# Dilated attention's 24 units, laid out as steps between the dense matmuls of two runs

## What is computed

```python
h = rms_norm(x, norm_w)
proj = h @ w_in
a_u, a_v, a_z, b_q, b_k, b_v, b_z, m_q, m_z, g = split(proj)
u = gelu(a_u); vv = layer_norm(gelu(a_v)); y_a = spatial_gating(u, vv) * silu(a_z)

q, k = rms_norm(b_q per head), rms_norm(b_k per head)
for gi, (window, dilation) in enumerate(((128, 1), (512, 4), (2048, 16))):
    # each query attends to t, t-d, ..., t-window; 4 heads of 64
    scores = q @ k.T * 64 ** -0.5 + bias[bucket(distance)]     # masked to the window
    m = max(scores); p = exp(scores - m); l = sum(p)
    o_g, lse_g = (p @ v) / l, m + log(l)
wts = softmax over the groups of lse
y_b = sum(wts * o_g) * silu(b_z)

kv = rms_norm(mem, mem_norm_w) @ m_w_kv          # 256 memory tokens
y_m = softmax(rms_norm(m_q) @ rms_norm(mk).T) @ mv * silu(m_z)
x = x + (gates[0]*(y_a@proj_a) + gates[1]*(y_b@proj_b) + gates[2]*(y_m@proj_m)) @ w_out
```

## Time and profile before

| | us |
|---|---|
| median of 3 runs (1761.26 to 1764.52) | 1763.2 |
| span of the profiled execution | 1759.4 |
| PE busy in it | 1726.5 (98%) |
| DVE busy | 914.9 (52%) |
| ACT busy | 654.1 (37%) |
| first run, up to the end of its gate slots | 0 to 262.7 |
| the stage of the 24 units | 262.7 to 326.4 |
| middle run from its first slot | from 326.4 |

### The profile page before, as it was taken

How to read it: one execution, slowest core, us unless ns; L and a number is a source line. 1 busy time by engine, 2 the same in 40 slices (tenths; PEclk the granted TensorE clock), 3 DMA queues, 4 the chain that set the end, 5 groups by cost and what they waited for, 6 DMA issues and landing times.

```text
span 1759.4 us, 22322 instructions
## 1 busy us (share of the span) xinstructions
PE 1726.5 (98%) x8731; PEld 1398.6 (79%) x8731; DVE 914.9 (52%) x1528; ACT 654.1 (37%) x1225; POOL 249.0 (14%) x412
## 2 busy tenths in 40 slices
PE   7999999999999999999999999999999999999998
PEld 5788887778888888778888788888887777777786
DVE  5158868664336744763222322467242545657764
ACT  5234438611324432752112211233313363434731
POOL 3012210188801100000000000482000000000000
PEclk9999999999999999999999999999999999999999
DMA  4121110346232200311111221242713111001132
GB/s 145 52 76 47 37 37 2 118 144 192 85 123 72 61 25 13 94 30 49 54 42 52 66 63 31 96 144 79 156 31 99 42 31 37 25 25 48 40 130 107
DMA packets 148339, 122.93 MB, mean 70 GB/s; under 512 B 10555, under 2 KB 133898, under 8 KB 147594
## 3 DMA queue, kind: packets, MB, share of 16 engines
q1 hardware_dynamic: 148234, 121.49, 22.9%
HBM read 108.21 MB, written 13.26 MB: 69 GB/s over the span
## 4 chain that ended last, share of the span: by engine, by line
PE 56%; DVE 2%; ACT 1%; issue 1%; DVEq 0%; ACTq 0%
PE psum L93 30%; PE psum L278 10%; PE psum L81 7%; PE psum L2707 2%; PE psum L2738 2%; PE psum L2721 1%; PE psum L1720 1%; PE psum L945 0%; PE psum L931 0%; PE psum L2503 0%; PE psum L2524 0%; PE psum L920 0%; PE psum L2217 0%; DVE ya_low L1572 0%; PE psum L1481 0%
## 5 line engine op out<-in xcount | busy, mean ns | idle before, releaser
L93 PE MATMUL psum<-hT,w_parts 128*128 128x512 f32 x3360 | 796.4, 393 | 7.1 <-PEq L61 3.4
L93 PEld LDWEIGHTS psum<-hT,w_parts 128*128 128x128 f32 x3360 | 629.3, 189 | 144.7 <-issue 8.9
L221 DVE TENSOR_TENSOR w_parts<-w_raw,w_parts 128x1024 fp32r<-128x1024 f32 x88 | 111.7, 1270 | 364.9 <-ACT w_parts L210 364.9
L93 PE MATMUL psum<-h2T,w_parts 128*128 128x512 f32 x1248 | 297.1, 394 | 0.0
L93 PEld LDWEIGHTS psum<-h2T,w_parts 128*128 128x128 f32 x1248 | 230.8, 188 | 48.3 <-issue 1.7
L1514 ACT ACTIVATE gate<-psum,cols 128x512 f32<-128x512 f32 x48 | 33.1, 689 | 284.1 <-PE psum L81 284.0
L81 PE MATMUL psum<-y_high,wp_parts 128*128 128x512 f32 x384 | 128.8, 395 | 0.3 <-DVE ya_low L1572 0.3
L210 ACT CAST w_parts<-w_raw 128x1024 fp32r<-128x1024 f32 x88 | 91.6, 1041 | 24.7 <-DMA w_raw<-w_in 19.5
L81 PEld LDWEIGHTS psum<-y_high,wp_parts 128*128 128x128 f32 x384 | 72.0, 188 | 18.9 <-DVE ya_low L1572 1.6
L278 PE MATMUL psum<-w_parts,y_parts 128*128 128x512 f32 x360 | 82.6, 390 | 0.6 <-DVE w_parts L271 0.6
L403 DVE RECIPROCAL x<-x 128x512 f32<-128x512 f32 x24 | 80.2, 3341 | 0.0
(11 more groups left out here) (377 smaller groups left out, 2298.5 us busy)
## 6 DMA issues: line engine op xcount, KB each, us to landing
w_raw<-w_in SPq DMA_DIRECT2D x188, 256.0 KB, 3.4
middle_a<-ada_w SPq DMA_DIRECT2D x32, 384.0 KB, 3.7
w_raw<-w_out SPq DMA_DIRECT2D x16, 512.0 KB, 3.8
qkT<-x SPq DMA_DIRECT2D x8, 512.0 KB, 7.9
w_raw<-m_w_kv SPq DMA_DIRECT2D x16, 256.0 KB, 3.1
base<-x SPq DMA_DIRECT2D x8, 512.0 KB, 4.0
x_kept<-x_ring SPq DMA_DIRECT2D x8, 512.0 KB, 3.8
base<-x_kept SPq DMA_DIRECT2D x8, 512.0 KB, 3.6
```

Source lines behind the costliest of these rows:

```text
L93: last = pe.matmul(out, lhs(a, k), rhs(b, k), start=(n == 0), stop=(n == len(SLOT) - 1))
L221: dve.tensor_tensor(self.parts[:, u, LO, :, :], self.raw[:, :, :], self.parts[:, u, HI, :, :].bitcast(F32), ALU.subtract).then_inc(self.lo ...
```

## The change

The units' stage is taken apart. What one round of it did (scores(b), turn(b-2), mix(b-3) on PE, and the parts of ACT and DVE) is now a "body" b, 0 to 26. `Dense` gets four places in a slot: after matmul 6, 12, 18 and 24. Bodies 0 to 14 stand in the gate slots 36 to 39 of the first run (from place 1 of slot 36), bodies 15 to 26 in slots 0, 1 and 2 of the middle run. With it:

- scores have one pair of banks, `(2,)` (banks 2 and 3), so that scores(b) waits for the maxima of b-1; there is one `pT`; the `p` buffers lie in `x1` and, later, in dead rows of `qkT`;
- the gate tiles keep to banks 0 and 1, the last key tile to 6 and 7;
- on DVE and ACT the bodies of places 0 to 2 stand ahead of everything else of their slot, that of place 3 behind it;
- the first tile of the middle run is split after the last slot of the first run's tile 18, in the run itself;
- `Join` starts at slot 3 and spreads one group a slot instead of one half; `Modulation` moves from slot 1 to 4, its sum from 19 to 22; `MemNorm` from 18 to 21 with 3 slots a step in place of 4; the inputs of `SsmMatrices` are loaded at slot 3, its save moves from 30 to 32;
- short tiles start one tile later, and the last two of them now stand together behind the last query tile.

```diff
@@ class Dense, tensor
-            slot_part(pe, out, lhs, rhs, range(8))
+            slot_part(pe, out, lhs, rhs, range(6))
+            for work in self.beside:
+                work.tensor_body(pe, s, 0)
+            slot_part(pe, out, lhs, rhs, range(6, 8))
...
                 work.tensor_mid(pe, s)
+                work.tensor_body(pe, s, 1)
...
                 before.after(pe, self, s - 1)
+            for work in self.beside:
+                work.tensor_body(pe, s, 2)
             last = slot_part(pe, out, lhs, rhs, range(18, 24))
@@ class Dense, scalar
         for s, slot in enumerate(self.slots):
...
+            for place in range(3):
+                for work in self.beside:
+                    work.scalar_body(act, s, place)
...
                 w.split_high(act, slot.n // 2 + 1, slot.n % 2)
+            elif slot.last and slot.n + 2 == len(self.tiles) and self.ahead:
+                self.ahead.ahead_high(act)
             for work in self.beside:
                 work.scalar(act, s)
+                work.scalar_body(act, s, 3)
@@ class Dense, vector
         for s, slot in enumerate(self.slots):
+            for place in range(3):
+                for work in self.beside:
+                    work.vector_body(dve, s, place)
...
                 w.split_low(dve, slot.n // 2 + 1, slot.n % 2)
+            elif slot.last and slot.n + 2 == len(self.tiles) and self.ahead:
+                self.ahead.ahead_low(dve)
             self.tiles[slot.n].vector(dve, self, s)
             if s:
                 self.tiles[self.slots[s - 1].n].vector_last(dve, self, s - 1)
             for work in self.beside:
                 work.vector(dve, s)
+                work.vector_body(dve, s, 3)
@@ class DilatedAttention
-        super().__init__(core, stack, units, ident, p, pT, (0, 2), 4, (6, 7), lag=2)
+        super().__init__(core, stack, units, ident, p[0], pT, (2,), 4, (6, 7), lag=2)
...
+    def body_pe(self, pe, b):
...
+            self.scores(pe, b)
...
+            self.turn(pe, b - lag)
...
+            self.mix(pe, b - lag - 1)
+
+    def body_act(self, act, b):
+        if 0 <= b - self.lag < self.n:
+            self.move_act(act, b - self.lag)
+        if b < self.n:
+            self.exps(act, b)
+
+    def body_dve(self, dve, b):
...
+        if 0 <= b - self.lag - 2:
+            self.store(dve, b - self.lag - 2)
+        if b < self.n:
+            self.maxima(dve, b)
+        if 0 <= b - self.lag < self.n:
+            self.move_dve(dve, b - self.lag)
@@ class DilatedBodies (new)
+    def body(self, s, place):
+        b = 4 * s + place - self.start
+        return self.first_body + b if b >= 0 and self.first_body + b < self.attention.bodies else None
@@ class Middle
-        for small, tile in zip(mvs[0:3] + mks, late + mqs):
+        for small, tile in zip(mvs[0:2] + mks, late + mqs):
             self.tiles += [small, tile]
-        self.tiles.append(mvs[3])
+        self.tiles += mvs[2:4]
```

More of the change, by code:

```diff
@@ L360, in scalar @@
         sq, high = run.sq[:, 0:self.width], run.sq_high[:, 0:self.width]
+        if q == 0 and run.heads_free:
+            act.wait_ge(*run.heads_free)
         if q >= 1:
@@ L517, in scalar @@
             work.scalar_start(act)
-        if self.heads:
+        if self.heads and not self.same_at:
             act.copy(self.same, self.same_from).then_inc(self.same_made, 1)
@@ L523, in scalar @@
             tile = self.tiles[slot.n]
+            if self.same_at and s == self.same_at:
+                act.copy(self.same, self.same_from).then_inc(self.same_made, 1)
+            for place in range(3):
+                for work in self.beside:
+                    work.scalar_body(act, s, place)
             for work in self.beside:
@@ L853, in tensor, with tensor_before @@
         last.then_inc(self.turned, 1)
+    def tensor_before(self, pe, s):
+        if s == self.run.first_slot(self.run.tiles.index(self.reuses)):
+            for side, kept in enumerate(self.kept):
+                pe.wait_ge(kept, (len(self.pairs) + 1 - side) // 2)
     def place(self, n):
@@ L917, in scores @@
             pe.wait_ge(self.maxed, u - before + 1)
-            pe.wait_ge(self.exped, u - before + 1)
+            if self.units[u - before]["bias"] is None:
+                pe.wait_ge(self.exped, u - before + 1)
         for h in range(4):
@@ L1053 @@
 class DilatedAttention(Attention):
-    def __init__(self, core, stack, units, ident, p, pT, w, before):
-        super().__init__(core, stack, units, ident, p, pT, (0, 2), 4, (6, 7), lag=2)
-        self.w, self.before = w, before
-        assert self.n % 3 == 0
-    def evicted(self, engine, banks):
-        for b in banks:
-            engine.wait_ge(self.before.free[b], max(slot.prior + 1 for slot in self.before.slots if slot.bank == b))
-    def sync_start(self, sp):
-        sp.wait_ge(self.before.w.low, 2 * len(self.before.tiles))
-        self.w.ahead_load(sp)
@@ L1117, in vector_early, with __init__, place, evicted @@
-    def vector_early(self, dve, s):
-        pass
-    def vector(self, dve, s):
-        pass
+    def __init__(self, core, stack, units, ident, p, pT, before, tabled):
+        super().__init__(core, stack, units, ident, p[0], pT, (2,), 4, (6, 7), lag=2)
+        self.places, self.before, self.tabled, self.bodies = p, before, tabled, self.n + self.lag + 1
+        self.ring = 3
+    def place(self, u):
+        return self.places[u // TT][u % self.ring]
+    def evicted(self, engine, b):
+        engine.wait_ge(self.before.free[b], max(slot.prior + 1 for slot in self.before.slots if slot.bank == b))
@@ L1182, with __init__ @@
     ROWS = 96
-    FIRST = 1
-    def __init__(self, core, places_dram, sel_dram, maxima, sums, oT, ybT, ident, room, room_at):
+    FIRST = 3
+    def __init__(self, core, places_dram, sel_dram, maxima, sums, oT, ybT, ident, room, room_at, dilated, loads):
+        self.dilated = dilated
         self.core, self.places_dram, self.sel_dram, self.ident = core, places_dram, sel_dram, ident
@@ L1244, in tensor @@
             pe.transpose(self.by_head(), self.m.rearrange("p g c -> p (g c)"), self.ident).then_inc(self.turned, 1)
[L1245 to L1246 removed]
+        if 2 <= s < 5:
+            g = s - 2
             rows = slice(32 * g, 32 * g + 32)
[L1248 removed]
+            if g == 0:
                 pe.wait_ge(self.chosen, 1)
                 pe.wait_ge(self.rest, 1)
[L1251 to L1259 removed]
+            for pair in range(2):
+                if g:
+                    pe.wait_ge(self.used, 2 * g + pair - 1)
+                for h in range(2):
+                    half = slice(h * HALF, (h + 1) * HALF)
+                    out = bank(self.core, 2 + 2 * pair + h, 1)
+                    pe.matmul(out, self.sel[rows, pair * P:(pair + 1) * P], self.high[rows, half],
+                              start=True, stop=False)
+                    last = pe.matmul(out, self.sel[rows, pair * P:(pair + 1) * P],
+                                     self.low[rows, half], start=False, stop=True)
+                last.then_inc(self.spread, 1)
     def vector_early(self, dve, s):
@@ L1357, in at @@
     def at(self, s, step):
-        t, k = divmod(s - self.first, 4)
-        return {0: t, 1: t - 1}[step // 4] if (k == step % 4 and 0 <= t - step // 4 < 2) else None
+        t, k = divmod(s - self.first - step, 3)
+        return t if k == 0 and 0 <= t < 2 else None
     def sync(self, sp, s):
@@ L3270, in first_block @@
                              1 / 64, order=by_group(rates[j // 2]), banks=four) for j in range(6)]
+            for where, tile in [((6, 7), keys[5])] + [((0, 1), tile) for tile in gates]:
+                tile.banks = (where, where)
             tiles = values + queries + keys + gates
@@ L3295, in first_block @@
         w_gates = SplitTiles(core, stack, [(24, lambda n: gate_tile(order[0], 0))], shares=w)
-        middle.prepare(w_middle, dilated, maxima, sums, oT, ybT, stat, w_gates)
+        middle.prepare(w_middle, dilated, last_bodies, maxima, sums, oT, ybT, stat, w_gates)
         run_dense(core, run, middle.run)
@@ L3373, in __init__ @@
                        for j in range(6)]
-        late, self.tiles = self.tiles[13:16], self.tiles[0:13]
+        late, self.tiles = self.tiles[14:16], self.tiles[0:14]
         for tile in late:
@@ L3390, in __init__, with prepare @@
                                wait=lambda h, j=j: self.turn_av.wait(2 * j + h)) for j in range(6)]
-    def prepare(self, w, dilated, maxima, sums, oT, ybT, stat, ahead):
+    def prepare(self, w, dilated, bodies, maxima, sums, oT, ybT, stat, ahead):
         core, A, later, mergedT, N = self.core, self.A, self.later, self.mergedT, SSM_GROUPS
```

196 lines of the change are left out of this document (102 added, 94 removed).

## The result

The changed kernel takes 1781.8 us (median of 4 runs, 1774.4 to 1784.8), the kernel before 1762.2 beside it (4 runs): ratio 1.011, 95% interval 1.0095 to 1.0126. Slower, by 19.6 us. The profiled execution of after has a span of 1781.1, 21.7 more than before's 1759.4; the prediction had 22.6.

What follows compares the result with a forecast made beforehand. PE, busy 1726.5 of 1759.4 us, was taken as the bound. Terms 0.2 + 8.4 + 2.8 + 2.6 + 3.1 + 1.7 + 3.8 = +22.6 gave span 1782.0, plus 3.8 to the runs' median: 1785.8 us, range 1771 to 1793.

Steps and rivals of the forecast that it cites:

- the clock: Behind the new waits: slow matmuls cost 3.8 us, ends 0 and 7.5; the first wait's share is in the 8.4.
- what I had put at nothing: Other moves, such as the later `SsmMatrices` save: shifts by whole slots that PE does not wait for, no term.
- The ledger: Units' stage on PE: spreading frees 4.9 us, 27 insertions of 0.19 add 5.1; +0.2 us, other end -4.9.
- The first gate slot: PE waits 4.1 us ahead of scores(1), 2.5 ahead of scores(3), for maxima delayed by DVE's reciprocals; +8.4 us in all.
- The splits of slot 37, of the start of the middle run and of slot 1: DVE's weight splits stand ahead of the maxima in these places; PE waits 2.8, 2.6 and 3.1 us.
- The short tiles: Two short tiles at the end: weights of the first `a_v` tile land late, PE waits 1.7 us.
- that sign: Gate slot 38 should take 24 x 0.2285 us plus 4 bodies with 0.19 each, and no wait.
- the case with waits only where no split makes them: Rival: only the reciprocal's 8.4, 0.75 of clock and the short tiles' 1.7 stay; +11.1, 1774.3 us; chance 12%.
- The wait-free case: Rival: maxima come in time everywhere; 1763.4 us, or 1758.3 if insertions cost nothing; chance 5%.
- The case of the clock that holds: Rival: dense matmuls ahead of each wait keep 2.4 GHz; +17.8, 1781.0 us, 1775.9 with free insertions; chance 15%.
- The function switch at twice its load: Rival: on ACT, a silu/exponential switch costs twice the table load, lengthening three split waits; +5.2, 1791.0 us; chance 5%.
- the late chain: Rival: `SsmMatrices` starts late, PE waits for the first memory key's sums; 3 to 8 us more, 1789 to 1794; chance 8%.

Runs made afterwards that it cites:

- experiment 8: Changed kernel, maxima first, short tiles apart, earlier reciprocal pair ahead of the split, low-part split behind body 4, last reciprocal halved: 1762.6 us, ratio 1.0003.
- Experiment 4: Changed kernel with 16 useless dense matmuls on PE just ahead of scores(1): 1778.0 us (one run).
- Experiment 1: Changed kernel with DVE taking the place-3 body ahead of split and reciprocal, the middle run's starting split behind its first body: 1772.5 us, ratio 1.0058.
- experiment 2: Changed kernel with a plain copy for the silu of both gate tiles and the middle run's first two tiles: 1770.6 us (one run).
- experiment 3: Changed kernel with the memory's third value tile ahead of the second late gate tile, one short tile left at the end: 1778.2 us (one run).
- experiments 6: Changed kernel with maxima first, short tiles apart, and in slot 35 the previous slot's reciprocal and product ahead of the split: 1766.1 us, ratio 1.0028.

## Why the prediction was right

The time lies 4 us under the forecast and well in the range; the mechanisms hold, and two terms were mis-sized, the clock and what I had put at nothing.

- **The ledger**, +0.2 forecast. Six dense matmuls behind a body take 269.57 - 267.99 = 1.58 in after's timeline instead of 1.37: 0.21 for an insertion against my 0.19, 5.5 us for the 26 more than before's one break. Freed were the 4.9 that I counted and about 0.7 more, since a narrow body takes 1.82 instead of 1.88. Near zero, as forecast; experiment 8 agrees with it as a whole.
- **The first gate slot**: waits of 4.1 and 2.5 forecast, 3.82 and 1.31 measured. The second is smaller because PE was slower before it: maxima(2) ended at 260.5, 0.9 later than in my sum, which is just the shift from the kernel's start; but PE arrived at 259.3, not at 257.1, 1.3 later than that shift gives. Experiment 4 shows the exchange directly.
- **The splits of slot 37, of the start of the middle run and of slot 1**: 2.8, 2.6 and 3.1 forecast, 2.51, 2.41 and 2.75 measured, each with `L230` just ahead of the released maxima. Each term is 0.2 to 0.35 too high. In slot 37, with T = 274.2, the maxima ended at T + 7.3 (7.5 in my sum) and PE wanted its scores at T + 4.8 (4.7). Experiment 1 removes all three by the queue, experiment 2 halves them or more by the table loads.
- **The short tiles**: 1.7 forecast, 2.06 measured. It was 1.28 and 1.20 in experiments 2 and 4, which changed nothing there, so it varies by some 0.8 us; in all of them ACT's cast starts when the DMA of the weights ends.
- **The clock**, the mis-sized term: 3.8, and 1.8 more inside the 8.4, together 5.6; the profiled run lost about 10.1 (2.9, 2.9, 2.7 and 1.6; nothing behind the 2.51). I priced a slow stretch at 1.5 from the one in before; three of these lasted longer. I also gave the `a_v` wait no clock loss, and it had one. The range held that.
- **What I had at nothing** came out at -3.5: fewer breaks of the dense stream by the join, the wait for `x`, the barrier and the modulation's sum, less the 0.9 at the start. Nothing of it was forecast, and it hid most of the miss on the clock. That the sum was closer than its terms is luck.

For slot 38 the prediction had written down 4 bodies and no wait. Taken by the letter that sign failed: the wait of 2.51 stands in it, ahead of its first body. By the prediction's own sum (T + 4.7, with T the end of slot 37) it had to stand there, so the sign contradicted the sum; the other three bodies, 8 to 10, have no wait. The rivals: the case with waits only where no split makes them is refuted by the three waits behind `L230`. The wait-free case needed another queue order, and experiment 8 comes near to that case, at its time (1762.6 against 1763.4). The case of the clock that holds may be true at times: one of the four runs took 1774.4 at 0.995, but that run has no trace. The function switch at twice its load and the late chain are not seen.

## What to carry to other kernels

When steps are put between dense matmuls, go through the in-order queue of each helping engine and ask of every piece ahead of the step's own: who waits for this, and when? A split that is wanted two slots later, standing ahead of maxima that are wanted now, costs its whole chain, and here changes of order, most of them on DVE, with one reciprocal cut in halves took back all 19.6 us. With fewer buffers the slack of a step is one turn of PE, so cut anything on DVE that is longer than that (a reciprocal of 3.35 us) into halves, and before moving a stage later look for the fixed deadline behind it.

## What the runs showed that I had not expected

When PE loses its clock for a wait, and for how long, is not decided by the length of the wait alone. All four waits of 3.8 us at the same place, behind the same matmuls, lost it, but not alike: in the profiled runs of after and experiment 1 the granted clock was 0.50 from the first of the matmuls behind on, and the place cost 2.9 us; in experiment 2 the scores behind ran at full clock, the grant fell over 1 us after PE had started again (0.55 in the window from 250.40), and it cost 1.6; in experiment 3 it fell in between and cost 1.5. The wait of 2.75 lost it at once in after (2.7) and about 1.5 us late in experiments 3 and 4. The wait of 2.51 kept it in after and experiment 4 and lost it, late, in experiment 3 (transposes and products behind at 1.70 and 1.98 instead of 1.09); 2.41 lost it in after, 2.40 kept it in experiment 4. Ahead of `a_v`, 2.06 lost it in after and 2.03 kept it in experiment 1. Even 1.92 and 1.97 lost it (experiments 6 and 1), and 1.93 kept it (experiment 3). So full-speed matmuls right behind a wait do not show that the clock held: look at the next few us too.

The runs of after spread over 10 us and follow their mean grant; those of experiment 8, whose waits are all short, spread over 4. The Trainium skill, page "TensorE: Matmul & The Clock Gate", section "Part 1: The HAM clock gate", says that the number of slow matmuls at a kernel's start varies between runs of one kernel. No kernel was profiled twice here, so the slow matmuls of two runs of one kernel can't be compared; what varies like that is the mean grant of after's runs, 0.990 to 0.995. What decides it in a given run, these runs do not show. For a forecast it means a term with two ends and not a number: nothing, or 1.5 to 3 us, for each wait like these.
